# Stick-breaking value product: high and low values side by side as one stationary side, two passes instead of three

## The reference

```python
def stick_breaking_attention(q, k, v):           # q, k, v (1, 512, 8, 64)
    def block(args):                              # one block of 128 queries
        z = jnp.einsum('bhqd,bhkd->bhqk', qblk, kh) * scale
        strict = kpos[None, :] < qp[:, None]
        log_beta = jax.nn.log_sigmoid(z)
        log_keep = jnp.where(strict, jax.nn.log_sigmoid(-z), 0.0)
        between = lax.cumsum(log_keep, axis=3, reverse=True) - log_keep
        w = jnp.where(strict, jnp.exp(log_beta + between), 0.0)
        return jnp.einsum('bhqk,bhkd->bhqd', w, vh)
# then: mixed = concat(sb_out, df_out);  x = x + mixed @ w_o
```

## Time and profile before

| | us |
|---|---|
| median of 3 runs | 2724.79 |
| lowest, highest | 2724.30, 2725.29 |
| profiled execution | 2724.33 |
| its span, first to last instruction | 2722.5 |
| PE, busy | 2691.4 (99%) |
| DVE, busy | 1582.8 (58%) |
| ACT, busy | 1151.8 (42%) |
| POOL, busy | 628.8 (23%) |

### The profile page before, as it was taken

The page is one execution under the profiler, slowest core; times in us unless marked ns, Lnnn a source line. Parts: engine busy times, 40 slices in busy tenths (PEclk is TensorE's granted clock), DMA queues, the critical chain, the costliest instruction groups (busy, mean ns, idle before and its releaser), DMA issues.

```text
span 2722.5 us, 31967 instructions
## 1 busy us (share of the span) xinstructions
PE 2691.4 (99%) x12918; PEld 2253.6 (83%) x12918; DVE 1582.8 (58%) x2307; ACT 1151.8 (42%) x1832; POOL 628.8 (23%) x401
## 2 busy tenths in 40 slices
PE   8999999999999999999999999999999999999998
PEld 6888888888888888888888888788888888788886
DVE  7656544444566646665575678744445668744444
ACT  4323323222347636533235767522224667522223
POOL 1000111011136625400005642411113451411100
PEclk9999999999999999999999999999999999999999
DMA  4232232332221222222222221233333221223332
GB/s 155 100 100 94 97 101 93 101 97 97 89 80 56 72 69 67 93 95 99 97 97 88 83 65 35 83 101 93 101 93 103 70 72 38 78 93 101 94 102 69
DMA packets 69412, 238.78 MB, mean 88 GB/s; under 512 B 7696, under 2 KB 10256, under 8 KB 69264
## 3 DMA queue, kind: packets, MB, share of 16 engines
q1 hardware_dynamic: 69264, 236.73, 27.5%
HBM read 234.60 MB, written 2.10 MB: 87 GB/s over the span
## 4 chain that ended last, share of the span: by engine, by line
PE 93%; DVE 4%; ACT 2%; issue 0%; DMA 0%; POOL 0%; SPq 0%; ACTq 0%; DVEq 0%
PE ps L414 30%; PE ps L415 29%; PE ps L416 29%; DVE ptl L1523 1%; PE ps L512 1%; PE ps L442 1%; ACT wh L899 0%; PE ps L460 0%; PE ps L461 0%; PE ps L735 0%; PE ps L734 0%; PE ps L466 0%; PE ps L572 0%; PE ps L573 0%; ACT pth L908 0%
## 5 line engine op out<-in xcount | busy, mean ns | idle before, releaser
L899 ACT ACTIVATE wh<-raw 128x1024 fp32r<-128x1024 f32 (+2 forms) x453 | 465.0, 1028 | 743.9 <-PE ps L416 739.1
L414 PE MATMUL ps<-xh,wh 128*128 128x512 f32 x1920 | 754.0, 393 | 0.0
L415 PE MATMUL ps<-xl,wh 128*128 128x512 f32 x1920 | 747.8, 389 | 0.0
L416 PE MATMUL ps<-xh,wl 128*128 128x512 f32 x1920 | 747.8, 389 | 0.0
L1515 DVE TENSOR_TENSOR wl<-raw,wh 128x1024 fp32r<-128x1024 f32 (+1 forms) x339 | 449.9, 1328 | 151.4 <-ACT wh L899 151.2
L414 PE MATMUL ps<-yh,wh 128*128 128x512 f32 x1088 | 425.1, 391 | 2.6 <-ACT t L927 1.6
L414 PEld LDWEIGHTS ps<-xh,wh 128*128 128x128 f32 x1920 | 360.9, 188 | 76.8 <-issue 2.4
L415 PE MATMUL ps<-yl,wh 128*128 128x512 f32 x1088 | 423.5, 389 | 0.0
L416 PE MATMUL ps<-yh,wl 128*128 128x512 f32 x1088 | 423.4, 389 | 0.0
L415 PEld LDWEIGHTS ps<-xl,wh 128*128 128x128 f32 x1920 | 360.9, 188 | 75.5 <-issue 2.2
L416 PEld LDWEIGHTS ps<-xh,wl 128*128 128x128 f32 x1920 | 360.7, 188 | 75.4
(11 more groups left out here) (255 smaller groups left out, 3646.7 us busy)
## 6 DMA issues: line engine op xcount, KB each, us to landing
raw<-in_ff SPq DMA_DIRECT2D x120, 512.0 KB, 3.6
raw<-in_pool_in SPq DMA_DIRECT2D x64, 512.0 KB, 3.3
raw<-in_conv_in SPq DMA_DIRECT2D x64, 512.0 KB, 3.3
raw<-in_pool_out SPq DMA_DIRECT2D x32, 512.0 KB, 3.3
raw<-in_qk SPq DMA_DIRECT2D x32, 512.0 KB, 3.6
raw<-in_pool_grp SPq DMA_DIRECT2D x16, 512.0 KB, 3.3
raw<-in_conv_out SPq DMA_DIRECT2D x16, 512.0 KB, 3.3
raw<-in_mla_z SPq DMA_DIRECT2D x16, 512.0 KB, 3.6
```

The source lines that it names most:

```text
L414: pe.do.matmul(o, lh, rh_, start=start, stop=False)
L415: pe.do.matmul(o, lh, rl_, start=False, stop=False)
L416: return pe.do.matmul(o, ll, rh_, start=False, stop=stop)
L899: act.do.activation(h[:, 0:ncol], r[:, 0:ncol], ACT.Copy).then_inc(*mark("whi", ("whi", k)))
```

## The change

For the stick-breaking heads, the values' high and low parts of one head are laid side by side, 64 and 64 columns, as one stationary side of 128 (the tiles G0 to G7 are now numbered by key block and half of the heads). A product is two passes, with the high and the low part of the weights, eight matmuls a head. The bank then holds the product with the high values in partitions 0 to 63 and that with the low values in 64 to 127. ACT copies the lower half to YL[p] (`sb_tail`), DVE adds it to the upper half in place in PSUM (`sb_sum`), and then `sb_out` of ACT and DVE make the high and the low part as before, from partitions 0 to 63. Each of the four steps waits for the one ahead of it. `sb_out` stands later in the order in most heads. In PE's order nine matmuls of `wo(1, 5)` (parts 0 to 2) move from the end of the output projection to the place right after `sb_pv(7)`.

```diff
--- before.py
+++ after.py
@@ -357,7 +357,11 @@
         def sqk(p):
             return (YH[2], YL[2], YH[3], YL[3]) if p == 1 else G[8:12]
 
-        VS = ((G[0:4], G[4:8]), (G[12:16], G[16:20]))
+        VS = (G[0:8], (G[12:16], G[16:20]))
+
+        def v_halves(kb, part):
+            v = VS[0][2 * kb + part][:, :].rearrange("p (h s c) -> p h s c", h=4, s=2)
+            return v[:, :, 0, :], v[:, :, 1, :]
         SA, SL, SBH, SBL = SETS[0]
         GA, GB, DFH, DFL = SETS[1]
         QH, QLO, KVH, KVL, KRH, KRL = G[0:3], G[3:6], G[6:8], G[8:10], G[10], G[11]
@@ -736,12 +740,15 @@
                         mm.then_inc(*mark("group", ("mm", "sb", l, h, kbs[0])))
 
                 def sb_pv(h):
-                    p = h // 2
-                    VH, VL = VS[0]
                     pe.wait_ge(*at("bpl", l, h, 0))
-                    pe.wait_ge(*at("vsl", l, 0, p // 2, 3))
-                    weigh_v((l, "s", h), slice(p * 128, p * 128 + 128), SBH, SBL,
-                            lambda kb, col: VH[kb][:, col], lambda kb, col: VL[kb][:, col])
+                    pe.wait_ge(*at("vsl", l, 0, h // 4, 3))
+                    b = bank("pv", l, "s", h)
+                    for kb in range(4):
+                        cc = slice(KOFF[kb], KOFF[kb] + 512 - 128 * kb)
+                        v = VS[0][2 * kb + h // 4][:, h % 4 * 128:h % 4 * 128 + 128]
+                        pe.do.matmul(b[:, kb * 128:512], v, SBH[:, cc], start=kb == 0, stop=False)
+                        mm = pe.do.matmul(b[:, kb * 128:512], v, SBL[:, cc], start=False, stop=kb == 3)
+                    mm.then_inc(*mark("group", ("mm", "pv", l, "s", h)))
 
                 def df_scores(h, base):
                     (q_h, q_l), (k_h, k_l) = dqk(h)
@@ -809,8 +816,8 @@
                 sb_between(6), wo(0, 6), sb_scores(7), sb_pv(6), df_squares(3), wo(1, 2, (0, 1))
                 wo(1, 1, (0, 1)), wo(0, 7), wo(1, 0, (0, 1))
                 sb_between(7), wo(1, 1, (2,)), wo(1, 4, (0, 1, 2)), wo(1, 3, (0, 1, 2)), sb_pv(7)
-                wo(1, 0, (2,)), wo(1, 2, (2,)), wo(1, 1, (3,)), wo(1, 0, (3,)), wo(1, 4, (3,)), wo(1, 2, (3,))
-                wo(1, 3, (3,)), wo(1, 5), wo(1, 7), wo(1, 6)
+                wo(1, 0, (2,)), wo(1, 2, (2,)), wo(1, 5, (0, 1, 2)), wo(1, 1, (3,)), wo(1, 0, (3,)), wo(1, 4, (3,))
+                wo(1, 2, (3,)), wo(1, 3, (3,)), wo(1, 5, (3,)), wo(1, 7), wo(1, 6)
                 first_pair(st + 1, [("f1", l, 0, 0), ("f1", l, 0, 1)], LAST_ROWS)
                 ring[0] = [home[i] for i in LAST_BANKS]
                 for qd in range(4):
@@ -1197,9 +1204,12 @@
                 def v_high(which, part):
                     for tb in range(4):
                         act.wait_ge(*at("rows", l))
-                        high(VS[which][0][tb][:, part * 256:part * 256 + 256],
-                             ps("v", l, which, part, tb // 2)[:, (tb % 2) * 256:(tb % 2) * 256 + 256],
-                             ("mm", "v", l, which, part, tb // 2), ("vsh", l, which, part, tb), small[:, tb:tb + 1])
+                        dst = VS[1][0][tb][:, part * 256:part * 256 + 256]
+                        src = ps("v", l, which, part, tb // 2)[:, (tb % 2) * 256:(tb % 2) * 256 + 256]
+                        if which == 0:
+                            dst, src = v_halves(tb, part)[0], src.rearrange("p (h c) -> p h c", h=4)
+                        high(dst, src, ("mm", "v", l, which, part, tb // 2), ("vsh", l, which, part, tb),
+                             small[:, tb:tb + 1])
 
                 def norms():
                     if l:
@@ -1266,12 +1276,17 @@
                             *mark("act", ("wexp", l, h, kbs[0])))
                         high(SBH[:, k0:k0 + n], SA[:, k0:k0 + n], ("wexp", l, h, kbs[0]), ("bph", l, h, kbs[0]))
 
+                def sb_tail(h):
+                    p, e = h // 2, h % 2
+                    if p == 3:
+                        act.wait_ge(*at("mm", "ds", l, 2, 16))
+                    high(YL[p][64 * e:64 * e + 64, :], ps("pv", l, "s", h)[64:128, :], ("mm", "pv", l, "s", h),
+                         ("pvtail", l, h))
+
                 def sb_out(h):
                     p, e = h // 2, h % 2
                     rr = slice(64 * e, 64 * e + 64)
-                    if p == 3:
-                        act.wait_ge(*at("mm", "ds", l, 2, 16))
-                    high(YH[p][rr, :], ps("pv", l, "s", h)[rr, :], ("mm", "pv", l, "s", h), ("yh", "wo", l, p, e))
+                    high(YH[p][rr, :], ps("pv", l, "s", h)[0:64, :], ("pvsum", l, h), ("yh", "wo", l, p, e))
 
                 def df_exp(h, base):
                     qbs = DF_QBS[base]
@@ -1337,8 +1352,9 @@
                 soft(1)
                 df_exp(0, 34)
                 keep(1)
+                sb_tail(0)
+                turned("dk", 1)
                 sb_out(0)
-                turned("dk", 1)
                 taking('sk', l, 1)
                 taking('dk', l, 2)
                 plain("sk", 1)
@@ -1357,9 +1373,10 @@
                 rot("dk", 2)
                 v_high(1, 1)
                 keep(2)
-                sb_out(1)
+                sb_tail(1)
                 taking('v', l, 1, 0, 0)
                 taking('v', l, 1, 0, 1)
+                sb_out(1)
                 df_exp(1, 34)
                 v_high(1, 0)
                 taking('dq', l, 2)
@@ -1372,8 +1389,9 @@
                 turned("dq", 2)
                 df_root(0)
                 turned("dq", 3)
+                sb_tail(2)
+                keep(3)
                 sb_out(2)
-                keep(3)
                 rot("dq", 2)
                 taking('sk', l, 2)
                 df_high(0)
@@ -1392,6 +1410,7 @@
                 turned("dk", 3)
                 df_root(1)
                 keep(4)
+                sb_tail(3)
                 taking('sq', l, 3)
                 df_turn(2)
                 sb_out(3)
@@ -1405,9 +1424,10 @@
                 soft(5)
                 df_exp(3, 32)
                 keep(5)
-                sb_out(4)
+                sb_tail(4)
                 taking('wo', l, 0, 0)
                 plain("sk", 3)
+                sb_out(4)
                 df_exp(3, 16)
                 weights_of(5)
                 df_root(2)
@@ -1416,8 +1436,9 @@
                 soft(6)
                 df_high(2)
                 keep(6)
+                sb_tail(5)
+                df_out(3)
                 sb_out(5)
-                df_out(3)
                 taking('wo', l, 0, 3)
                 taking('wo', l, 0, 2)
                 weights_of(6)
@@ -1425,9 +1446,11 @@
                 soft(7)
                 df_high(3)
                 keep(7)
+                sb_tail(6)
                 taking('wo', l, 1, 0)
                 sb_out(6)
                 weights_of(7)
+                sb_tail(7)
                 sb_out(7)
                 taking('wo', l, 1, 1)
                 x_high(st + 1, 1)
@@ -1937,9 +1960,12 @@
                 def v_low(which, part):
                     for tb in range(4):
                         cc = slice(part * 256, part * 256 + 256)
-                        low_scaled(VS[which][1][tb][:, cc],
-                                   ps("v", l, which, part, tb // 2)[:, (tb % 2) * 256:(tb % 2) * 256 + 256],
-                                   VS[which][0][tb][:, cc], small[:, tb:tb + 1], ("vsh", l, which, part, tb | 1),
+                        h, dst = [v[tb][:, cc] for v in VS[1]]
+                        src = ps("v", l, which, part, tb // 2)[:, (tb % 2) * 256:(tb % 2) * 256 + 256]
+                        if which == 0:
+                            h, dst = v_halves(tb, part)
+                            src = src.rearrange("p (h c) -> p h c", h=4)
+                        low_scaled(dst, src, h, small[:, tb:tb + 1], ("vsh", l, which, part, tb | 1),
                                    ("vsl", l, which, part, tb),
                                    *([("psfree", "v", l, which, part, tb // 2)] if tb % 2 else []))
 
@@ -1995,10 +2021,17 @@
                         low(SBL[:, k0:k0 + n], SA[:, k0:k0 + n], SBH[:, k0:k0 + n], ("bph", l, h, kbs[0]),
                             ("bpl", l, h, kbs[0]))
 
+                def sb_sum(h):
+                    p, e = h // 2, h % 2
+                    b = ps("pv", l, "s", h)
+                    dve.wait_ge(*at("pvtail", l, h))
+                    dve.do.tensor_tensor(b[0:64, :], b[0:64, :], f(YL[p][64 * e:64 * e + 64, :]), ALU.add).then_inc(
+                        *mark("dve", ("pvsum", l, h)))
+
                 def sb_out(h):
                     p, e = h // 2, h % 2
                     rr = slice(64 * e, 64 * e + 64)
-                    low(YL[p][rr, :], ps("pv", l, "s", h)[rr, :], YH[p][rr, :], ("yh", "wo", l, p, e),
+                    low(YL[p][rr, :], ps("pv", l, "s", h)[0:64, :], YH[p][rr, :], ("yh", "wo", l, p, e),
                         ("yl", "wo", l, p) if e else ("ylx", l, p), ("psfree", "pv", l, "s", h))
 
                 def df_max(h, base):
```

(16 more changed lines are left out.)

## The result

| | us |
|---|---|
| kernel before, median of 10 runs | 2724.69 |
| changed kernel, median of 10 runs | 2732.01 (2729.76 to 2733.87) |
| ratio, 95% interval | 1.0027 (1.0019 to 1.0035) |
| profiled execution after, its span | 2730.94, 2729.1 |

The change makes the kernel slower by 7.3 us. I had forecast 2725.9 us and a range up to 2730. The profiled executions differ by 6.6 us, and that is what the traces can explain.

What follows compares the result with a forecast made beforehand. PE, with matmuls under way for 99% of the span, was the bound. Gains and delays by head left layer 0 0.86 us late and layer 1 0.26, together 1.1 us more: 2725.9 us against the median, range 2722.5 to 2729.

Steps and rivals of the forecast that it cites:

- The bound and the worth of a pass: Attention of both second-block layers: PE bounds; removing a pass gives 0.62 us a head, 9.9 us over sixteen heads.
- Heads 0 to 2, 4 and 5: Heads 0 to 2 keep 1.86 us a layer, head 4 keeps 0.62, head 5's 0.62 becomes waiting.
- the end of the layer: After head 7's product: moved matmuls delay weight copy and POOL's splits, 1.61 us late; without the move 1.35.
- The add: DVE's 64x512 add in PSUM (`sb_sum`): 0.68 us each, bounds 0.59 and 1.16, never held by GpSimd.
- The pieces of 64 columns: Value split writing 64-column pieces: no added time, bounds 0 and 0.1 us each for 32 instructions, off PE's path.
- Head 3 in layer 0: Add and later `sb_out(3)` delay POOL's split, which holds the low half of df-k 3: 1.2 us later.
- then, with head 6's own 0.62: Head 6: its group comes 1.2 us later, then its product gives 0.62, leaving PE 0.70 and 1.30 us early.
- my own signs: Profile after: among others, first ff1 unit within 1.5 us of before; wrong if PE keeps over 1 us a layer past `wo`.
- Head 3, layer 1: Low half of df-k 3 is already held by the split there, so the new steps cost only 0.6 us.
- The copies are hidden after all: Rival: DVE's idle time takes the copies, most of the 9.9 us stays, 2715 to 2719 us; chance 0.14.
- Slower by held steps: Rival: two more two-input DVE steps a layer held by splits, 6.8 us on top of 1.1, 2732 us; chance 0.12.
- The change doesn't do what it says: Rival: shorter product costs as much as before, stationary sides load faster than PE takes them, 2733 us; chance 0.04.

Runs made afterwards that it cites:

- the wait filled: Changed kernel with six 512-column matmuls belonging to no result put on PE ahead of its wait for head 6's weights: 2727.65 us.
- none moved: Nine matmuls of wo(1, 5) back at the end of the output projection: changed kernel 2729.32 us; with heads 3 and 6 also relieved 2720.04 us.
- three passes: Changed kernel with a third pass put back in each product (high weights done twice), copies, add and orders as changed: 2740.15 us.
- head 3 relieved: Changed kernel with head 3's DVE add put behind the rotation of df-k 3 and ACT's high half behind that of df 1: 2726.69 us.
- before with three more copies: Kernel before, with ACT copying head 5's high half three times more before head 6's two weight copies: 2728.78 us.
- without copies: Changed kernel without the ACT copy and DVE add, high and low parts made straight from partitions 0 to 63, nine matmuls still moved: 2723.22 us.
- passes alone: Changed kernel without the ACT copy and the DVE add, and with wo(1, 5) not moved: 2720.34 us.
- filled (both): Six matmuls of no result ahead of PE's head 6 wait, in the changed kernel (2727.65 us) and in before with three more copies (2725.92 us).
- head 6 relieved: Changed kernel with head 5's DVE add after the low half of df 2 and its ACT high half after the two weight copies: 2725.82 us.
- six moved: Changed kernel with heads 3 and 6 relieved and only six of the nine matmuls of wo(1, 5) moved: 2719.27 us.

## Why the prediction was wrong

*Right.* The bound and the worth of a pass: head 2's eight matmuls start at 1606.35 and the next work at 1607.56, 1.21 us as forecast within 0.03. Heads 0 to 2, 4 and 5, and the end of the layer (1.61 forecast, 1.66 measured; 1.35 forecast without the move, 1.34 to 1.36 measured) came as worked out. The add took what I chose for it, 0.68 us; the line's view of the changed kernel:

```profile
L2028 DVE TENSOR_TENSOR ps<-ps,yl x16: 679/688/692, 1536.5 to 2351.3; 64x512 f32<-64x512 f32 x16
```

Not one of the sixteen was held, which agrees with the rule that I cited from the Trainium skill ("SBUF — State Buffer", Who interferes with whom): it reads SBUF once. The pieces of 64 columns cost the value split nothing (0.473 us a copy against 0.474), as I had taken. Head 3 in layer 0 has the mechanism that I described, the low half of df-k 3 held for 2.86 us until POOL's split ends:

```profile
1650.41 2.84 POOL L2331 TENSOR_TENSOR wl<-raw,wh 128x1024 fp32r<-128x1024 f32 x1 [3.58 <-ACT wh L906]
...
1650.93 2.86 DVE L1546 TENSOR_TENSOR yl<-t,yh 128x512 fp32r<-128x512 f32 x1
```

*The step that failed* is "then, with head 6's own 0.62". I let the whole group at head 6 come 1.2 us later, took the 0.62 us off behind it, and went on. It came 1.56 us later: ACT's wait grew by 0.85 (1.73 against 0.88, the add and a hand-over) and `sb_out(5)` is 0.59. That is a term a little too small. But a longer wait on PE was, in my working, no more than its length: the clock behind it I put at nothing, without a reason. After 1.92 us of waiting the work behind the product ran at half clock (in layer 1 the product too), so that in place of -0.62 stand +1.42 and +2.40 us. No rival of mine had the clock in it, although show the 1.00 on which every duration of PE rested. With the wait filled the kernel takes 2727.65 us, inside my range and 1.8 us above the forecast. Of my own signs two failed: the first ff1 unit comes 2.3 to 2.9 us later than before, not within 1.5, and PE keeps over 1 us a layer past the end of `wo` (2.7 and 3.7 us of the table).

*Head 3, layer 1:* 0.60 forecast, 1.69 measured. There too PE waited and then ran at 0.50 for 6.8 us. In the kernel with none moved, whose clock did not fall there, the same place cost 0.7 us. That this is so near to 0.60 is in part luck: the fall at 2251 that only before has lies inside this row. It puts PE 1.1 us ahead of before, and since the chain of head 3 hangs on DVE, PE waits that much longer (its two waits grow by 1.3 us each, by 0.6 and 0.8 in layer 0). So the price of the place itself is nearer to layer 0's 1.57 us, and my 0.6 for layer 1 ("this is so already") was too small.

*The reading of the whole.* I treated the pass as mostly kept and the copies as nearly free, and netted them. Passes: 8.1 us in place. Other edits: 15.5 us on a kernel with three passes. Neither is small. Moving the added steps of heads 3, 6 and 7 alone took 11.2 us off (2732.01 to 2720.77): what costs is where they stand.

*Rivals.* "The copies are hidden after all" names what the kernel could be (2719 to 2721 once they stand better), not what it is. "Slower by held steps" gave 2732, the measured time, by another mechanism: no held step beyond the one forecast is in PE's waits after. "The change doesn't do what it says" gave 2733, and the 1.21 us of head 2 rule it out. That either time fits is no support for it.

## What to carry to other kernels

A step added to ACT or DVE costs by what is queued behind it: put it behind the low half, the weight copy or the split that PE waits for next, and it can be free; ahead of it, it costs its whole length. In a kernel like this one, price a longer wait of TensorE twice, once as itself and once as the clock that may fall after it, and look at the granted clock of the stretch before a wait is called small. Work moved to cover a wait puts off whatever it releases; count that too.

## What the runs showed of the hardware

The granted clock after head 6, two passages for each kernel (layer 0 and layer 1), by how long PE stood still right ahead of the product:

| PE's wait ahead of head 6's product | kernels | passages with a fall to 0.50 there |
|---|---|---|
| 1.92 to 1.94 us | changed; three passes; none moved; head 3 relieved | 7 of 8 |
| 1.38 and 1.39 us | before with three more copies | 2 of 2 |
| 1.09 to 1.12 us | without copies; passes alone | 1 of 4 |
| up to 0.55 us | before; filled (both); head 6 relieved (alone and in three others) | 1 of 14 |

The stretches at 0.50 lasted 3.4 to 10.2 us. A wait makes a fall likely and does not decide it: with 1.94 us the layer 0 of the kernel with none moved kept its 1.00 (the stretch from 1704). Twelve of the 23 falls in the attention parts of all fourteen traces are not in this table:

- At head 3, two waits of 1.1 and 1.5 us stand 3 us apart in four kernels (changed, head 6 filled, head 6 relieved, none moved). Both passages of the first two have a fall there, both of the other two have none: 4 of 8. With three passes, waits of 1.0 to 1.5 us there were followed by none in 2. With six moved one more fell, in layer 1 (2267.8, behind a wait of 1.13 us).
- Seven falls of 3.4 to 6.8 us begin 2.5 to 3.2 us behind the first of the matmuls `ps<-g` of 64 rows, ahead of which PE had waited only 0.3 us (0.8 in the kernel with the passes alone): 2251.0 in before, 2259.7 with three passes, 1628.7 and 2249.9 with head 3 relieved, 1629.5 with six moved, 1630.9 and 2248.7 with the passes alone. That is 7 of 28 passages of this place, and what sets them off is not shown.
- At the end of a layer, waits of 1.3 us for the copies (none moved, in two kernels) were followed by no fall in 4 of 4.

So the table holds for its place. That the wait at head 6 is a cause and not a sign there rests on the two filled kernels. Stretches of the kernel with none moved, layer 0 and layer 1:

```profile
1704.00:1712.00 8.00, 6.39 (x28) 4.79 (x29) 4.80 (x11) 4.69 (x11) 0.00 (x0) 1.00 0.22 75
2324.39:2334.63 10.24, 7.93 (x18) 5.47 (x19) 5.08 (x10) 4.22 (x10) 0.46 (x1) 0.50 0.25 76
```

I had not expected waits of under 2 us, in a stretch where PE is busy for 94% of the time (113.16 of 120 us), to cost more by the clock behind them than by their own length: 2.0 and 3.0 us against the 1.56 us by which the waits grew.
